# Turning the probabilities of a prompt attention six steps behind their scores instead of five

## What is computed

```python
def diff_attend(q, k, v, q_pos, k_pos, lam):
    s = jnp.einsum('ntkgch,nskch->nkgcts', q, k, preferred_element_type=jnp.float32) * SCALE
    mask = k_pos[None, :] <= q_pos[:, None]
    s = jnp.where(mask, s, -jnp.inf)
    p = jax.nn.softmax(s, axis=-1)
    a = p[:, :, :, 0] - lam * p[:, :, :, 1]
    return jnp.einsum('nkgts,nskv->ntkgv', a, v.astype(jnp.float32))
```

## Time and profile before

| | |
|---|---|
| median of 3 runs | 2429.37 us (2425.97 to 2432.26) |
| profiled execution | 2426.89 us |
| its span | 2425.1 us |
| prompt attention | 1455 to 2020 us of the span |
| busy in the span | PE 90%, DVE 49%, ACT 42%, POOL 55% |
| mean granted TensorE clock | 0.913 |

### The profile page before, as it was taken

One profiled execution on the slowest core, in us unless ns is written; L12 is line 12 of the kernel. 1 busy time (PEld: TensorE's weight loads), 2 busy tenths in 40 slices (PEclk: granted clock), 3 DMA queues, 4 the chain that ended last, 5 costly groups with the idle time before them and its releaser, 6 DMA issues. The chain is left out here.

```text
span 2425.1 us, 38429 instructions
## 1 busy us (share of the span) xinstructions
PE 2174.6 (90%) x13067; PEld 1971.4 (81%) x13067; DVE 1182.8 (49%) x2195; ACT 1028.4 (42%) x1957; POOL 1343.2 (55%) x810
## 2 busy tenths in 40 slices
PE   5999999999349999999889988989898888898998
PEld 5999999999349998999889985766666666666998
DVE  4789889889883003222100006666666663346001
ACT  5555555555563112111221127766766773224111
POOL 3799999999744324433311227776676762225233
PEclk8999999999669999999999997877887887998999
DMA  7121222121224232222232331000010005882221
GB/s 247 45 71 52 61 61 61 44 70 52 88 72 124 62 115 71 79 70 92 76 97 89 105 114 45 18 29 17 18 36 9 10 1 175 258 266 67 62 79 72
DMA packets 182055, 192.69 MB, mean 79 GB/s; under 512 B 11434, under 2 KB 147059, under 8 KB 181331
## 3 DMA queue, kind: packets, MB, share of 16 engines
q1 hardware_dynamic: 181952, 191.48, 25.0%
HBM read 145.52 MB, written 47.63 MB: 80 GB/s over the span
## 5 line engine op out<-in xcount | busy, mean ns | idle before, releaser
L222 POOL TENSOR_TENSOR w_lo<-w_raw,w_hi 128x1024 fp32r<-128x1024 f32 x116 | 279.5, 2411 | 599.2 <-ACT w_hi L218 599.2
L242 PE MATMUL ps<-Hhi,w_hi 128*128 128x352 f32 x1704 | 560.1, 329 | 18.7 <-POOL w_lo L222 12.1
L242 PE MATMUL ps<-Hhi,w_lo 128*128 128x352 f32 x1704 | 549.9, 323 | 0.0
L242 PE MATMUL ps<-Hlo,w_hi 128*128 128x352 f32 x1704 | 548.9, 322 | 0.0
L788 DVE SCALAR_TENSOR_TENSOR ps<-U,dww,ps 128x512 f32<-128x512 f32 x608 | 403.0, 744 | 0.0
L218 ACT ACTIVATE w_hi<-w_raw 128x1024 fp32r<-128x1024 f32 x116 | 122.1, 1053 | 661.4 <-PE ps L242 244.4
L702 POOL TENSOR_TENSOR pool_acc<-pool_acc,prod 128x1024 f32<-128x1024 f32 x144 | 346.2, 2404 | 31.0 <-ACT prod L651 22.7
L242 PEld LDWEIGHTS ps<-Hhi,w_hi 128*128 128x128 f32 x1704 | 321.5, 189 | 28.4 <-POOL w_lo L222 18.8
L242 PEld LDWEIGHTS ps<-Hlo,w_hi 128*128 128x128 f32 x1704 | 322.4, 189 | 2.3 <-issue 0.2
L242 PEld LDWEIGHTS ps<-Hhi,w_lo 128*128 128x128 f32 x1704 | 321.4, 189 | 0.0
L651 ACT ACTIVATE prod<-U,dww 128x1024 f32<-128x1024 f32 x176 | 197.0, 1147 | 249.7 <-POOL pool_acc L702 143.2
(11 more groups left out here) (249 smaller groups left out, 4012.2 us busy)
## 6 DMA issues: line engine op xcount, KB each, us to landing
w_raw<-conv_w_in SPq DMA_DIRECT2D x48, 512.0 KB, 4.1
w_raw<-attn_w_in SPq DMA_DIRECT2D x40, 512.0 KB, 4.5
kpage<-cache_k SPq DMA_DIRECT2D x64, 256.0 KB, 3.0
vpage<-cache_v SPq DMA_DIRECT2D x64, 256.0 KB
res<-Y SPq DMA_DIRECT2D x2, 4224.0 KB, 16.8
gate<-sg SPq DMA_DIRECT2D x16, 528.0 KB, 4.0
sgl<-gate SPq DMA_DIRECT2D x16, 528.0 KB, 4.5
xres<-res SPq DMA_DIRECT2D x16, 528.0 KB, 3.9
```

What stands on the lines that cost most here:

```text
L222: pool.tensor_tensor(wlo[s][:, :, :], raw[s][:, :, :], whi[s][:, :, :].bitcast(F32), ALU.subtract).then_inc(w_lo, 1)
L242: mm = pe.matmul(ps[:, 3 * dst + c, 0:CH], w[:, k, :], r(k)[:, c * CH:(c + 1) * CH], start=start and k == 0 and w is whi[s] and r is rhs_h ...
```

## The change

LAG goes from 5 to 6: a unit's blocks are turned, split and, further on, used one step later. The tables that say at which step values, outputs, column sums and their copies come are shifted by one with it, and so is the step at which the new group's values are split (NEW_VALUES, 9 to 10). NEXT_Q stays. PRE and TAIL, the steps ahead of and behind the loop, follow from the tables and go from 14 to 15.

```diff
@@ -1476,15 +1476,15 @@
         NX = GH * QT
-        LAG = 5
+        LAG = 6
 
 
         UNITS = 12
         NU = UNITS * GH
-        VALUES = {12: (0, (0,)), 13: (0, (1, 2)), 14: (0, (3,)),
-                  17: (1, (0, 1)), 18: (1, (2, 3)), 19: (1, (4, 5)), 20: (1, (6, 7))}
-        OUTPUTS, TOTALS, SUMS = {15: 0, 21: 1}, {18: 0, 24: 1}, {19: 0, 25: 1}
-        NEW_VALUES, NEXT_Q = 9, 1
+        VALUES = {13: (0, (0,)), 14: (0, (1, 2)), 15: (0, (3,)),
+                  18: (1, (0, 1)), 19: (1, (2, 3)), 20: (1, (4, 5)), 21: (1, (6, 7))}
+        OUTPUTS, TOTALS, SUMS = {16: 0, 22: 1}, {19: 0, 25: 1}, {20: 0, 26: 1}
+        NEW_VALUES, NEXT_Q = 10, 1
         PRE = max(SUMS) - UNITS + 1
```

## The result

| | before | after |
|---|---|---|
| median of 4 runs each on one chip | 2428.38 us (2425.97 to 2432.26) | 2413.93 us (2411.87 to 2417.45) |
| profiled execution, span | 2426.9, 2425.1 us | 2414.2, 2412.4 us |
| first to last scores of the prompt attention | 545.2 us | 529.9 us |
| granted clock in it | 0.81 | 0.84 |

The ratio is 0.9939 with an interval of [0.9927, 0.9951]: 14.5 us faster, 0.61%. That is the side that was forecast, inside the forecast's own range of 2385 to 2420, and half of the 30 us that the sum gave.

The account below looks back on a forecast made before the run. PE was taken as the bound, idling for POOL's joined probabilities (39.7 us) and partly at its lower clock. 10 us from the walk plus 20 from the clock gave 30 us, so 2400 us; range 2362 to 2442, the forecast's own 2385 to 2420.

Parts of the forecast that it names:

- The POOL wait goes: At unit 6's turn in each head, PE's 2.28 us wait for POOL's join of chunk 5 goes.
- The walk within the head: From unit 10's scores to the next head's unit 1: new waits 0.35, 0.8, 1.35 us; 0.7 us won a head, 10 us.
- "I take 0" for the groups' ends: Late scores of a new group waiting for the keys' low part: up to 1.0 us more, three times; taken as 0.
- The loop's start "nothing": Prologue and epilogue one step longer, loop starting one step later: at most a fill and a drain step, counted as nothing.
- The clock: PE's clock falling after the wait in each head: kept in 5 heads at 4 us, 20 us; bounds 0 to 60.
- The clock up nearly everywhere: Rival, prompt attention's heads: clock kept in 10 to 15 heads at 4 us, 2360 to 2380 us; chance 0.20.
- The even trade: Rival, each head: bank and unit 11's exponentials hold PE as long as POOL did, clock falls everywhere; 2422 to 2436, chance 0.18.
- A second fall at steps 5 and 6: Rival: light steps drop the clock again in a third to half of heads, 4.5 us each; 2441 to 2453, chance 0.22.
- POOL under 8: Sign in PE's waits: the wait for POOL's join goes from about 40 us to under 8.
- DVE 20 to 30: Sign in PE's waits: the wait for DVE's low parts rises from 14 to 20 or 30 us.
- New waits for ACT ahead of unit 1: Sign on PE: new waits for ACT's exponentials ahead of the scores of unit 1; the walk had 1.35 us.
- Clock of a group 0.82 to 0.88: Sign in the prompt attention: granted clock of a group of four heads at 0.82 to 0.88.

Follow-up runs that it names:

- experiment 1: Kernel before with only the turn (and high and low parts) one step later, values, outputs and sums at their old steps: 2435.04 us, 1.0028 to before.
- experiment 2: Kernel before with only the tables (values, outputs, sums, split of new values) one step later, LAG still 5: 2451.54 us, 1.0098 to before.
- experiment 3: The change with the first half's values, output and sums and NEW_VALUES back at their old steps: 2431.0 us, 1.0007 to before.
- experiment 4: The change with PRE one more, so the loop starts and jumps back one step later: 2418.44 us, 0.9952 to before.
- experiment 5: Kernel before with the scores of unit 11 issued ahead of the turn of unit 6 on PE: 2401.34 us, 0.9887 to before.
- experiment 8: The change with eight useless matmuls a head, four ahead of unit 6's turn, four ahead of unit 1's scores: 2390.73 us, 0.9836 to before.
- experiment 9: Kernel before with sixteen useless matmuls a head ahead of the turn of unit 6: 2413.18 us, 0.9934 to before.
- experiment 6: The change with DVE's low part of a unit ahead of the coefficients in every step: 2415.01 us, 0.9938 to before.
- experiment 7: The change with the next group's keys made in two halves of 512 columns, the first one unit earlier: 2407.0 us, 0.9911 to before.
- experiment 12: The change with keys in halves and seventeen useless matmuls a head: 2368.46 us, 0.9764 to before.
- experiment 10: The change with keys in halves and eight useless matmuls a head together: 2382.44 us, 0.9810 to before.

## Why the prediction was half right

**The POOL wait goes: right.** 39.7 to 0.7 us, the join done 1.6 us ahead of its turn.

**The walk within the head: right, a little too dark.** Its three waits came to 0.16 + 0.91 + 0.81 = 1.9 us instead of 2.5. Over the stage, POOL −39.0, DVE +13.7 and ACT +11.0 make −14.3 us. The wait for the low part of the values fell by 3.4 us more, which was not forecast. The sum's "10 us" for this walk does not follow from it: 2.5 us of waits for 2.28 at the same work and clock make a head 0.2 us longer, not 0.7 shorter; by the walk's own numbers the lead at the scores of unit 0 is lost again ahead of those of unit 1. And the 15 waits and "three small ones" of the prediction are 18 of 1.6 to 2.3 us: one of the three stands in the first head and two at the end of the stage, and they are not small.

**"I take 0" for the groups' ends: the step that failed.** I let the three values matmuls and the earlier scores of unit 11 cancel and bounded the cost at 1.0 us more a group. It was 3.4 us more, 4.4 in all:

```profile
1575.61 0.66 PE L1597 MATMUL ps<-small,p 128*128 128x128 f32 x4 [0.91 <-DVE aTlo L1790]
...
1580.67 0.47 PE L1581 MATMUL ps<-khi,qhi 64*128 64x128 f32 x2 [4.40 <-DVE klo L1237]
```

In this timeline of PE the turn of unit 6 is followed by nothing for 4.4 us. Counted from the scores of unit 10, PE now comes to the late scores 4.3 us behind, not 8.3: the waits on the way are 0.16 and 0.91 us for 2.28, the clock is still high, and the three values matmuls are gone. The keys are ready at 8.5 us, not 9.1. So PE is 4.0 us sooner and the keys only 0.6. DVE's copy of their low part does begin 2.2 us sooner, but it takes 1.6 us longer. Before, it began just as POOL's join of chunk 6 had ended (timeline of POOL and DVE):

```profile
1581.61 2.10 POOL L1835 TENSOR_TENSOR p<-p,p 128x896 f32<-128x896 f32 x1
...
1583.78 1.23 DVE L1237 TENSOR_TENSOR klo<-kraw,khi 128x1024 fp32r<-128x1024 f32 x1
```

In the change it begins 0.34 us behind the join's start, and takes 2.82 us for the same 1024 columns:

```profile
1577.29 2.07 POOL L1835 TENSOR_TENSOR p<-p,p 128x896 f32<-128x896 f32 x1
...
1577.63 2.82 DVE L1237 TENSOR_TENSOR klo<-kraw,khi 128x1024 fp32r<-128x1024 f32 x1 [0.69 <-ACT khi L1660]
```

Its end, 1580.45, is 1.09 us behind the join's end, 1579.36. In all eight kernels in which it began behind this join's start and ahead of its end (the change and experiments 1, 2, 3, 4, 5, 8 and 9) it ended 1.08 or 1.09 us behind the join's end, whether it took 2.26 or 2.83 us. So it does its work only when the join is over. In experiment 6 the copy happens to begin first, and there the join is the one that is held:

```profile
1578.57 1.27 DVE L1237 TENSOR_TENSOR klo<-kraw,khi 128x1024 fp32r<-128x1024 f32 x1 [0.67 <-ACT khi L1660]
1578.86 2.92 POOL L1835 TENSOR_TENSOR p<-p,p 128x896 f32<-128x896 f32 x1
```

The copy takes 1.27 us, the join 2.92 instead of 2.07, and the late scores wait 3.5 us instead of 4.4. The low parts of the turned blocks, which DVE reads from PSUM, keep their 0.69 us. The slower copy is 1.6 (2.82 − 1.23) of the 3.4 us a group. I had read the key copy's place in the order and not what POOL does at that time. Halved and partly drawn ahead of the join (experiment 7), the copies take 1.05 and 0.68 us, and the wait is 1.1 at the longest. The three values matmuls account for 0.7 us (experiment 3, where the copy takes 2.81).

**The loop's start "nothing": failed, small.** The loop jumps back at another step, and there PE and ACT stand without work for 2.2 to 2.8 us, twice, 5.1 us. Before, no such row stood in PE's list of waits; ACT already had two such idles, of 1.5 and 1.4 us. Experiment 4 moved the idle with the jump, but won nothing that could be measured.

**The net of the waits.** −14.3 − 3.4 + 10.2 + 5.1, and 1.6 for the small ones, is −0.8 us, where the sum had −10. The two terms that were taken as nothing, 15.3 us together, took back what the walk had won. So nearly all of the result came from the other term, the clock, and that the time still lies in the forecast's range is owed to the width of the range and not to the sum.

**The clock: right in kind, somewhat too large.** Low time fell by 39.6 us. At the 0.45 of the earlier trace rows (4.6 of 10.3) that is up to 17.7 us; PE's busy time in the stage fell by 11.6 us at the same matmuls, and its time without work by 3.7. So the clock brought 12 us of the stage's 15.3 or more, against 20 forecast. The price was right: 4 us for a head that keeps the clock, and heads 6 and 2 above differ by 4.2. The picture of "a third of the heads, 5, kept" was wrong in form: two heads lost the low stretch and eight had a shorter one. Behind the key wait it stayed at 13.7 to 17.1 us, and in the two heads with the jump a second one followed, 17.1 us in all. The fall also moved. Before, it came at units 10 and 11 at the end of all fifteen heads, inside POOL's wait or just behind it. Now it comes inside the 4.4 us key wait at the three groups' ends. At the twelve other head ends PE waits 0.9 and then 0.8 us (in some heads in three parts), and the clock falls there, at units 0 and 1 of the next head, in ten. Into heads 6 and 10 it does not fall, though the waits ahead of them are the same to 0.02 us as those ahead of head 7, where it does. The clock ahead of such a fall, behind it, and over the same two waits without one:

```profile
1676.00:1683.60 7.60, 5.65 (x40) 3.72 (x39) 6.38 (x18) 6.03 (x19) 6.33 (x8) 1.00 0.00 1
1684.50:1694.00 9.50, 9.50 (x40) 7.77 (x39) 3.86 (x15) 5.25 (x17) 7.63 (x10) 0.50 0.01 2
1651.50:1656.50 5.00, 3.19 (x24) 2.40 (x25) 3.64 (x17) 4.67 (x17) 4.16 (x4) 1.00 0.01 2
```

Single waits far under the 2.28 us of the earlier trace rows, close together, can be enough; that is where I was too hopeful in weighing them against the 0.64 that is survived. What decides between two heads with the same waits stays open, so that it was two heads and not five is not explained by the waits.

The sum had 30 us; in the profiled executions the span fell 12.7 (2425.1 to 2412.4) and the stage 15.3. The 3 us between them are lost behind the stage, where the code is the same; the cause was not tried and stays open.

**The rivals.** The clock up nearly everywhere (2360 to 2380) did not come by this change alone, but experiment 12 reached it with 2368. The even trade was right about the waits (75.3 for 76.1) and wrong about the time, because the clock gained. The Trainium skill (Perfetto Trace Analysis, Optimization Strategy) reads a gap that repeats as a possible lack of room in SBUF or PSUM. Taken so, the bubble should have moved to the bank. Of its 39.0 us, 13.7 did, and 11.0 moved to the exponentials; no bank was added, and POOL's gap is gone, so the trace agrees with it for a third of the gap at most. A second fall at steps 5 and 6 was not seen in the change: the only falls early in a head, at unit 2 of two heads, stand at the jump. In experiments 1 and 3 short low stretches of 3.4 us do begin at units 5 and 6, in seven and eight heads, so that rival was not far off.

**The signs.** POOL under 8: 0.7. DVE 20 to 30: 28.0. New waits for ACT ahead of unit 1: yes. Clock of a group 0.82 to 0.88: 0.85 and 0.86. All as named; what was missing from the list is the key wait.

## What to carry to other kernels

- When a wait on the bounding engine is removed, walk on to the next thing that it needs from elsewhere, and look at what the other engines do at the new time; where that thing does not come sooner by itself, the wait is handed on. Here 3.4 us at each of three group ends took back 10.2 of the 17.7 us that the other waits had given.
- Where the granted clock is below 1.00, split a stage's time into heads or tiles with and without a low stretch before pricing a change, and compare heads with the same work and the same waits: 28.4 us against 32.6 was a larger effect than the 1.9 us of waits in a head. Which wait stands just ahead of each fall says where to work.
- A lag and its tables belong together: either half of this change alone was slower than before.

## What was unexpected of the hardware

- **Work that computes nothing made the kernel faster.** Eight matmuls of 128 columns a head gave 23 us, seventeen with the keys in halves 45 us, for the most part by the granted clock (0.84 to 0.87 and 0.93). The order of before with sixteen gained as much (15 us) as the change.
- **DVE and POOL wait for each other inside an instruction.** DVE's subtraction of two operands in SBUF took 1.23 us alone and 2.26 to 2.83 when POOL's join had begun first, always ending 1.08 or 1.09 us behind it. When DVE began first (experiment 6), it took 1.27 us and the join 2.92 instead of 2.07. No semaphore shows this, only the length. The Trainium skill (SBUF — State Buffer, SBUF: two separate sides) says that such a DVE operation and a GpSimd one lock a shared pair of ports for a whole instruction, so that the later one blocks; the traces agree, in both directions.
- **Short waits lower the clock too.** Around 0.9 + 0.8 us, about two microseconds apart, it fell at ten of the twelve head ends that have no longer wait, and at two with the same waits it did not; each 0.64 us wait by itself is survived. The Trainium skill (TensorE: Matmul & The Clock Gate, on a second failure mode) tells of short idles between groups of matmuls that make the clock go up and down; here the trace agrees, with these numbers.
- **The jump back of a loop is not free**: in the change it left 2.78 us idle on PE and 2.18 on ACT, and 3.03 on ACT when it was moved by a step. In the order of before the jump left PE no idle, and ACT a shorter one:

```profile
1630.49 0.49 ACT L1695 ACTIVATE aThi<-ps 128x384 fp32r<-128x384 f32 x1 [1.47 <-issue]
```

In experiments 8, 10 and 12, with filler (useless matmuls) on PE, the jump falls on the same step as in the change, and there too ACT has the idle (2.2 to 2.3 us) and PE has none. So the step that it falls on matters, and something besides it that these runs do not show.
